# One decoder step on one core: the first tile's experts chosen in three parts, and two of its query products ahead of the other tile's layer norm

## The chip, the cores and the metric

The kernel runs on 1 core of one Trainium2 chip. A core has five engines with instruction streams of their own: TensorE (PE; PEld are its weight loads), VectorE (DVE), ScalarE (ACT), GpSimd (POOL) and SyncE (SP). They meet only at semaphores, and each runs its own list strictly in order. The metric is the device time of one execution in microseconds (us), as the median of several runs.

## The reference

Input are 512 tokens of a prompt and 8 sequences of 8 new tokens, 576 rows of 1024 float32 numbers. One layer is computed: a token mixer (a state-space branch and a sliding-window attention branch, gated and added), then a layer norm, then PEER, a layer with 16,384 experts, then a second layer norm. What matters here is the end of the mixer and PEER:

```
x1 = layer_norm(ALPHA * x + merged @ w_out)
q  = x1 @ peer_wq                      # 8 heads, two halves of 64 each
s1, s2 = q_half1 . k1, q_half2 . k2    # 128 scores each, per token and head
v1, i1 = top_k(s1, 16);  v2, i2 = top_k(s2, 16)
sc, sel = top_k(v1[:, None] + v2[None, :], 16)     # of the 256 pairs
idx, gate = i1 * 128 + i2 at sel, softmax(sc)      # 16 experts per head
h   = peer_u[idx] . x1                 # 8 * 16 = 128 rows of 1024 per token
out = sum(gelu(h) * gate * peer_v[idx])
x2 = layer_norm(ALPHA * x1 + out)
```

So each token fetches 128 rows of `peer_u` and 128 rows of `peer_v`, each of 4 KB.

## The kernel before, in words

**Tiles.** Tile 0 holds the 64 new tokens, tiles 1 to 4 hold 128 prompt tokens each. Tiles 1 and 0 form group 0, whose mixer runs first; tiles 2, 3, 4 form group 1, whose mixer runs while the experts of tiles 1 and 0 are worked on. PEER takes the tiles in the order 1, 0, 2, 3, 4.

**Slots.** A slot is one expert per token. Per slot GpSimd issues one indirect DMA for 128 rows of `peer_u` (`u_row`, L500) and one for `peer_v` (`v_row`, L507), 0.5 MB each, the latter four slots later. Tile 0 is folded onto 128 partitions and has 64 slots, the others have 128: 576 slots in all. VectorE makes the dot product of a u row (L1221), ScalarE the GELU for four slots together (L1471) and a diagonal matrix per slot (L1465), and TensorE adds diagonal times v row into banks 6 and 7 (`weigh`, L795). For a share of the slots VectorE adds the v row itself (L1208, L1211). Four slots make one item `("peer", t, c)`. A u row's place is free again after its dot product, and for the first 72 slots there are 6 places for u rows and 9 for v rows.

**Choosing.** `("sc", t, i)` are the score products of four heads on TensorE (L778), `("top", t, h)` the search for the 16 best pairs of one head on VectorE (L1121 to L1153), and `("choose", t, part)` turns four heads' results into expert numbers and gates on VectorE (L1161 to L1180), with one exponential on ScalarE. `choose` raises the semaphore `idx_s`; GpSimd waits for it before slot 0 and before slot 64 of a tile.

**Order.** `schedule()` writes one list of items, and every engine takes its own work from it in that order (TensorE and part of ScalarE take `peer` items later, behind the items that follow them: `mixer_first`). So the list fixes, on each in-order engine, what stands behind what. Before the first expert it reads: the output product of both tiles (`wo`, L747; on VectorE L1094 and the layer norm, L1078 to L1085), the transposes of the normed tiles (`xt`, L757), four query products for both tiles together (`wq`, L766, 192 columns; ScalarE copies each out, L1271), the scores of the first four heads, the other four query products, four searches, the scores of the second half, and `choose` for 64 slots. After that the list interleaves peer items with group 1: its three query-key-value products (`qkv`, L639 and, on VectorE, L979 to L990), transposes (`turn`, L647), attention scores and their softmax (`s`, L696 and L1042), probabilities times values (`pv`, L713 and L1051), gates, merge, output product and queries.

**Weights.** SyncE loads 104 pieces of 0.5 MB in order of use into a ring of 8 places (L426); a piece waits until the piece that is 8 before it has been used for the last time.

## Time and profile before

| | us |
|---|---|
| median of 3 runs | 2177.97 |
| lowest and highest of them | 2165.36, 2591.91 |
| the profiled execution | 2157.18 |
| span of its instructions | 2155.4 |

| engine | busy us | share of the span |
|---|---|---|
| PE | 1581.4 | 73% |
| DVE | 1370.7 | 64% |
| POOL | 1343.8 | 62% |
| ACT | 387.1 | 18% |

The 16 DMA engines moved 675.05 MB, 609.25 of them in GpSimd's queue (the expert rows and a few small transfers). To read it: the shares are means over stages that differ. Until 347 us no expert row is fetched; from then to the end the expert rows are. The page's line of DMA shares in 40 slices (of 53.9 us each) reads 5234346967999987999899999999989999999997.

### The profile page before, as it was taken

How to read it: one execution, taken by the hardware profiler on the slowest of the kernel's cores; microseconds unless marked ns; L12 is line 12 of the kernel's file. 1: busy time of each engine (PE TensorE's matmuls, PEld its weight loads, DVE VectorE, ACT ScalarE, POOL GpSimd, SP SyncE). 2: the span in 40 equal slices, each digit the busy share in tenths (PEclk: the TensorE clock that was granted, in tenths of full speed). 3: DMA queues.
4: the chain of work that ended last, by engine and by line, in shares of the span. 5: the costliest groups of instructions: out<-in, count | busy, mean ns of one | idle time of the engine just before them, and what ended most of it. 6: DMA issues, size and time to landing. Idle time of an engine off the chain costs nothing.

```text
span 2155.4 us, 16267 instructions
## 1 busy us (share of the span) xinstructions
PE 1581.4 (73%) x4705; PEld 797.3 (37%) x4705; DVE 1370.7 (64%) x3118; ACT 387.1 (18%) x905; POOL 1343.8 (62%) x1370
## 2 busy tenths in 40 slices
PE   6979986776987786876677675766675767776766
PEld 4667853444544332421232232322232322222222
DVE  7551237978989689858775666654476656444444
ACT  0222211223323122001111111111011121111111
POOL 0064004646667665777677777777777777667774
PEclk9979998878998898898889797989887889999998
DMA  5234346967999987999899999999989999999997
GB/s 213 90 78 119 124 141 219 347 216 267 356 367 379 373 310 272 400 351 370 292 371 373 356 371 358 364 383 367 391 328 357 358 356 389 367 362 373 380 369 269
DMA packets 186552, 675.05 MB, mean 313 GB/s; under 512 B 20960, under 2 KB 23440, under 8 KB 186048
## 3 DMA queue, kind: packets, MB, share of 16 engines
q0 software_dynamic: 167056, 609.25, 75.9%
q1 hardware_dynamic: 17632, 59.51, 7.7%
q10 hardware_dynamic: 1776, 5.24, 0.6%
q8 instruction: 39, 0.64, 0.1%
q14 instruction: 49, 0.40, 0.1%
HBM read 669.71 MB, written 3.69 MB: 312 GB/s over the span
## 4 chain that ended last, share of the span: by engine, by line
PE 29%; POOL 20%; issue 18%; DVE 15%; DMA 13%; another core or an unknown queue 2%; ACT 2%; ACTq 0%; SPq 0%; POOLq 0%; DVEq 0%
PE bank L795 15%; POOL region L507 7%; POOL region L500 6%; DMA region<-in_pv,region 6%; PE bank L726 4%; POOL wring L500 4%; DVE region L1221 2%; DMA discretisation<-in_pv,region 2%; DVE region L1211 2%; DMA wring<-in_pv,region 1%; DMA wring<-in_pu,region 1%; PE bank L547 1%; DMA region<-in_pu,region 1%; PE bank L747 1%
## 5 line engine op out<-in xcount | busy, mean ns | idle before, releaser
L795 PE MATMUL bank<-region,small 128*128 128x512 f32 (+1 forms) x1296 | 653.4, 650 | 281.3 <-ACT small L1465 123.0
L500 POOL DMA_INDIRECT region<-in_pu,region x348 | 390.6, 1122 | 292.2 <-DVE region L1221 103.4
L1221 DVE CUSTOM_DVE_ANT_0 region<-region 128x1024 f32<-128x1024 f32 x348 | 424.3, 1227 | 224.8 <-DMA region<-in_pu,region 199.3
L507 POOL DMA_INDIRECT region<-in_pv,region x392 | 442.5, 1129 | 163.3 <-issue 114.0
L795 PEld LDWEIGHTS bank<-region,small 128*128 128x128 f32 (+1 forms) x1296 | 248.8, 202 | 667.0 <-issue 546.0
L1221 DVE CUSTOM_DVE_ANT_0 wring<-wring,region 128x1024 f32<-128x1024 f32 x228 | 276.9, 1226 | 216.0 <-DMA wring<-in_pu,region 186.5
L500 POOL DMA_INDIRECT wring<-in_pu,region x228 | 238.4, 1046 | 69.5 <-issue 69.2
L1465 ACT ACTIVATE small<-small,region 128x128 f32<-128x128 f32 (+1 forms) x480 | 157.2, 387 | 667.5 <-DVE region L1195 241.3
L795 PE MATMUL bank<-discretisation,small 128*128 128x512 f32 (+1 forms) x196 | 117.9, 733 | 124.1 <-issue 65.4
L795 PE MATMUL bank<-wring,small 128*128 128x512 f32 x256 | 119.1, 599 | 22.7 <-DMA wring<-in_pv,region 15.4
L726 PE MATMUL bank<-xT,wring 128*128 128x192 f32 (+1 forms) x512 | 130.7, 417 | 0.0
L1471 ACT ACTIVATE region<-region 128x4 f32<-128x4 f32 x144 | 29.4, 204 | 519.2 <-issue 253.3
L726 PEld LDWEIGHTS bank<-xT,wring 128*128 128x128 f32 x512 | 94.2, 198 | 39.1 <-issue 7.3
L795 PEld LDWEIGHTS bank<-discretisation,small 128*128 128x128 f32 (+1 forms) x196 | 38.8, 213 | 188.5 <-issue 126.8
L1211 DVE SCALAR_TENSOR_TENSOR region<-region 128x1024 f32<-128x1024 f32 x66 | 84.9, 1287 | 18.4 <-issue 17.1
L795 PE MATMUL bank<-small 128*128 128x512 f32 (+1 forms) x172 | 87.6, 634 | 11.4 <-DMA small<-in_pv,region 7.2
L507 POOL DMA_INDIRECT small<-in_pv,region x60 | 68.8, 1146 | 26.1 <-issue 18.8
L507 POOL DMA_INDIRECT wring<-in_pv,region x64 | 69.9, 1093 | 19.5 <-issue 17.1
L507 POOL DMA_INDIRECT discretisation<-in_pv,region x60 | 65.3, 1089 | 25.0 <-issue 14.6
L795 PEld LDWEIGHTS bank<-wring,small 128*128 128x128 f32 x256 | 46.7, 190 | 91.7 <-issue 90.5
L747 PE MATMUL bank<-wring,region 128*128 128x512 f32 (+1 forms) x160 | 72.4, 612 | 9.3 <-DVE region L1069 9.3
L766 PE MATMUL bank<-xT,wring 128*128 128x192 f32 (+1 forms) x256 | 69.7, 433 | 1.4 <-ACT xT L1271 1.4
(244 smaller groups left out, 1709.8 us busy)
## 6 DMA issues: line engine op xcount, KB each, us to landing
wring<-in_w SPq DMA_DIRECT2D x104, 512.0 KB
region<-in_pv,region POOLq DMA_INDIRECT x392
region<-in_pu,region POOLq DMA_INDIRECT x348
wring<-in_pu,region POOLq DMA_INDIRECT x228
out_y<-region ACTq DMA_DIRECT2D x4, 512.0 KB
small<-in_small ACTq DMA_DIRECT2D x1, 1669.0 KB, 14.2
xT<-in_xT SPq DMA_DIRECT2D x1, 1536.0 KB, 20.0
region<-in_x SPq DMA_DIRECT2D x3, 512.0 KB, 16.7
```

The lines of the kernel that those rows point to most:

```text
L500: pool.indirect_dma_start(ring_u[u_at.place[q]], None, io["pu"], bass.IndirectOffsetOnAxis(ind[:, k:k + 1], 0)).then_inc(g_u[u_at.place[q] ...
L507: pool.indirect_dma_start(ring_v[v_at.place[q]], None, io["pv"], bass.IndirectOffsetOnAxis(ind[:, k:k + 1], 0)).then_inc(g_v[v_at.place[q] ...
L547: last = mm(b[:, 0:cn], w[:, k, :], xT[:, k, c0:c0 + cn], start=k == 0, stop=k == KT - 1)
L726: last = mm(b[:, 0:cn], w[:, k0 + k, :], src[:, k, s0:s0 + cn], start=k == 0, stop=k == kn - 1)
L747: last = mm(b[0:tn, :], mTg[g][:, k, rel(t):rel(t) + tn], w[:, 512 * hf:512 * hf + 512], start=k == 0, stop=k == KT - 1)
L766: last = mm(b[:, 0:cn], w[:, k, :], xT[:, k, c0:c0 + cn], start=k == 0, stop=k == KT - 1)
L795: last = mm(bank[6 + hf][0:tn, :], diag[:, d % DIAGS, 0:tn], ring_v[v_at.place[q]][:, 512 * hf:512 * hf + 512], start=k == 0, stop=t not i ...
L1211: V.scalar_tensor_tensor(out=acc, in0=ring_v[v_at.place[q]], scalar=aact[:, n % 2, k:k + 1], in1=acc, op0=ALU.mult, op1=ALU.add).then_inc( ...
L1221: V.tensor_tensor_reduce(out=ring_u[u_at.place[q]], in0=ring_u[u_at.place[q]], in1=x1[t], scale=1.0, scalar=0.0, op0=ALU.mult, op1=ALU.add ...
L1465: S.activation(diag[:, d % DIAGS, 0:tn], eye, ACT.Copy, scale=aact[:, n % 2, k:k + 1]).then_inc(diag_s, 1)
L1471: S.activation(hact[:, n % 2, k], hdot[:, n % 2, k], ACT.Gelu).then_inc(act_s, 1)
```

## The change

The first tile (tile 1) chooses its experts in three parts, of heads 0 and 1, 2 and 3, and 4 to 7, in place of two of four heads. The query products of heads 0 and 1 are made in two pieces: `wqf` for the 128 columns of tile 1, right after its transposes, and `wql` for the 64 columns of tile 0, after its own. The item `wo` is cut into one per half and an item `ln`; tile 0's second output half, its layer norm, transposes and all further query products now stand behind the first `choose` in the list. The weights of the first two query heads get two places of their own (in the region that later holds v rows), and the ring of 8 carries the rest. GpSimd waits before slots 0, 32 and 64 of tile 1. Searches 2 to 7 and two `choose` items of tile 1 now stand between its peer items.

```diff
+CHOICES = {1: [(0, 2), (2, 4), (4, 8)]}
+AHEAD = 2
+AHEAD_PLACES = 7
...
-    s += [("wo", 1), ("wo", 0), ("xt", 1), ("xt", 0)] + [("wq", 0, h) for h in range(4)] + [("sc", 1, 0)]
-    s += [("wq", 0, h) for h in range(4, 8)]
-    s += [("top", 1, h) for h in range(4)] + [("sc", 1, 1), ("choose", 1, 0)]
-
-    first = [[("top", 1, h)] for h in range(4, 8)] + [[("choose", 1, 1)]]
+    s += [("wo", 1, 0), ("wo", 1, 1), ("ln", 1), ("wo", 0, 0), ("xt", 1)] + [("wqf", h) for h in range(AHEAD)] + [("sc", 1, 0), ("wo", 0, 1)]
+    s += [("top", 1, 0), ("top", 1, 1), ("choose", 1, 0), ("ln", 0), ("xt", 0)] + [("wql", h) for h in range(AHEAD)]
+    s += [("wq", 0, 2), ("wq", 0, 3), ("sc", 1, 1)] + [("wq", 0, h) for h in range(4, 8)]
+
+    first = [[("top", 1, 2)], [("top", 1, 3), ("sc", 1, 2)], [("choose", 1, 1)]] + [[("top", 1, h)] for h in range(4, 8)] + [[("choose", 1, 2)]]
...
-                if i >= PIECES:
-                    sp.wait_ge(filled, plan.filled[plan.last_use[pieces[i - PIECES]]])
+                if before_in_slot[p]:
+                    sp.wait_ge(filled, plan.filled[plan.last_use[before_in_slot[p]]])
+                elif p in ahead:
+                    wait_item(sp, ("ht",))
...
-                    if k == 0:
-
-                        pool.wait_ge(idx_s, 2 * n + (2 if t == 0 else 1))
-                    if k == 64:
-                        pool.wait_ge(idx_s, 2 * n + 2)
+                    if t == 0 and k == 0:
+
+                        pool.wait_ge(idx_s, chosen(0, 1))
+                    for p, (h0, h1) in enumerate(choices(t)):
+                        if t and k == TOPK * h0:
+                            pool.wait_ge(idx_s, chosen(t, p))
...
                     if v_at.before[q] is not None:
                         wait_v_used(pool, v_at.before[q])
+                    elif v_at.place[q] in range(AHEAD_PLACES, AHEAD_PLACES + AHEAD):
+                        pool.wait_ge(filled, plan.filled[("wql", AHEAD - 1)])
...
+            def do_wqf(h):
+
+                after(("xt", 1, 1))
+                b = enter(("wqf", h))
+                w = arrived(0, "wq", h).rearrange("p (k n) -> p k n", k=8)
+                for k in range(KT):
+                    last = mm(b[:, 0:128], w[:, k, :], xT[:, k, 64:192], start=k == 0, stop=k == KT - 1)
+                last.then_inc(filled, 1)
...
-            def do_wo(t):
-                tn = TILES[t][1]
-                dve.wait_ge(x2_in if t > 1 else x_in, 16 * len(GROUPS[group(t)]))
-                dve.wait_ge(ln_in, 16)
...
+            def do_wo(t, hf):
+                if hf == 0:
+                    dve.wait_ge(x2_in if t > 1 else x_in, 16 * len(GROUPS[group(t)]))
+                    wo_half(t, 0)
+
+            def do_ln(t):
+                wo_half(t, 1)
+                dve.wait_ge(ln_in, 16)
+                tn = TILES[t][1]
                 layer_norm(x1[t][0:tn, :], x1[t][0:tn, :], tn, ln1).then_inc(x1_s, 1)
...
-                heads, half = slice(4 * part, 4 * part + 4), slice(64 * part, 64 * part + 64)
+                h0, h1 = choices(t)[part]
+                nh, nk, heads, half = h1 - h0, TOPK * (h1 - h0), slice(h0, h1), slice(TOPK * h0, TOPK * h1)
...
-                    step(V.tensor_tensor(eq[0:tn], posf[0:tn, side, half].unsqueeze(2).broadcast_to([tn, 64, TOPK]),
-                                         s("iota")[0:tn].unsqueeze(1).broadcast_to([tn, 64, TOPK]), ALU.is_equal))
+                    step(V.tensor_tensor(same, posf[0:tn, side, half].unsqueeze(2).broadcast_to([tn, nk, TOPK]),
+                                         s("iota")[0:tn].unsqueeze(1).broadcast_to([tn, nk, TOPK]), ALU.is_equal))
...
+            def do_wqf(h):
+                b = full(("wqf", h))
+                drain(("wqf", h), copy(q2T(1, h), b[:, 0:128]))
```

What the list does to the engines' orders is shown at two places. The first is TensorE, from the output products to the end of the qkv products. Before (L747 `wo`, L757 `xt`, L766 `wq`, L778 `sc`, L639 `qkv`, L795 `weigh`):

```order
L747 MATMUL bank<-wring,region 128x512 x16
L747 MATMUL bank<-wring,region 64x512 x16
L757 MATMUL bank<-small,region 128x128 x8
L757 MATMUL bank<-small,region 128x64 x8
L766 MATMUL bank<-xT,wring 128x192 x32
L778 MATMUL bank<-small,region 128x128 x8
L766 MATMUL bank<-xT,wring 128x192 x32
L778 MATMUL bank<-small,region 128x128 x8
L639 MATMUL bank<-wring,xT 128x512 x8
L639 MATMUL bank<-wring,xT 128x256 x8
L795 MATMUL bank<-region,small 128x512 x8
L639 MATMUL bank<-wring,xT 128x512 x8
```

Changed (L783 `wo`, L793 `xt`, L811 `wqf`, L820 `wql`, L802 `wq`, L833 `sc`, L676 `qkv`, L850 `weigh`):

```order
L783 MATMUL bank<-wring,region 64x512 x8
L793 MATMUL bank<-small,region 128x128 x8
L811 MATMUL bank<-xT,region 128x128 x16
L833 MATMUL bank<-small,region 128x128 x4
L783 MATMUL bank<-wring,region 64x512 x8
L793 MATMUL bank<-small,region 128x64 x8
L820 MATMUL bank<-xT,region 128x64 x16
L802 MATMUL bank<-xT,wring 128x192 x16
L833 MATMUL bank<-small,region 128x128 x4
L802 MATMUL bank<-xT,wring 128x192 x32
L676 MATMUL bank<-wring,xT 128x512 x8
L676 MATMUL bank<-wring,xT 128x256 x8
```

Two heads' queries and four score products come ahead; the transposes of tile 0, and with them all other query products and the three `qkv`, come behind the layer norm that VectorE makes after its first `choose`. Between the first and the second `qkv` there now stand 8 score products (`("sc", 1, 2)`), which wait until VectorE has read the two banks in its fourth search.

The second place is ScalarE, around the first GELU of the experts. Before (L1410 the square root of a layer norm, L1271 copies, L1435 the exponential of `choose`, L1471 the GELU):

```order
L1271 ACTIVATE hgT<-bank 128x64
L1271 ACTIVATE region<-bank 128x128
L1435 ACT_TABLE_LOAD
L1435 ACTIVATE region<-region 128x64
L1471 ACT_TABLE_LOAD
L1471 ACTIVATE region<-region 128x4
```

Changed (L1475 the square root, L1336 copies, L1509 the exponential, L1545 the GELU; eight more rows of copies are left out):

```order
L1509 ACT_TABLE_LOAD
L1509 ACTIVATE region<-region 128x32
L1475 ACT_TABLE_LOAD
L1475 ACTIVATE stat<-stat 64x1
L1336 ACTIVATE xT<-bank 128x4x64 x2
L1336 ACTIVATE hgT<-bank 128x64 x3
...
L1336 ACTIVATE hgT<-bank 128x64
L1336 ACTIVATE region<-bank 128x128
L1545 ACT_TABLE_LOAD
L1545 ACTIVATE region<-region 128x4
```

The exponential of the first `choose` now stands ahead of the copies of tile 0 and of the later queries, and the first GELU behind all of them.

## Rows read from the trace of the kernel before

**Rows 1.** Windows: busy us of PE, PEld, DVE, ACT, POOL, clock, DMA share, GB/s.

```profile
347.00:539.00 192.00, 135.34 (x419) 79.79 (x418) 150.94 (x323) 45.80 (x89) 116.38 (x101) 0.80 0.79 287
539.00:755.00 216.00, 176.14 (x497) 95.69 (x495) 189.03 (x404) 58.19 (x82) 142.83 (x124) 0.91 0.98 369
1037.00:2155.00 1118.00, 771.58 (x1615) 308.18 (x1613) 643.46 (x1484) 167.42 (x505) 830.05 (x765) 0.88 0.96 362
```

**Rows 2.** Timeline, GpSimd: start us, us, instruction, [idle before <- what ended it].

```profile
347.47 1.04 POOL L500 DMA_INDIRECT region<-in_pu,region  x1 [81.55 <-DVE region L1180]
```

**Rows 3.** Timeline, VectorE, from the first layer norm to the first dot product.

```profile
278.99 0.69 DVE L1094 SCALAR_TENSOR_TENSOR region<-region,bank 128x512 f32<-128x512 f32 x1 [5.57 <-PE bank L747]
...
285.47 1.22 DVE L1085 TENSOR_TENSOR region<-region 128x1024 f32<-128x1024 f32 x1
...
316.94 0.50 DVE L1121 MAX8 region<-bank 128x8 f32<-128x128 f32 x2 [17.78 <-PE bank L778]
...
336.72 0.23 DVE L1161 TENSOR_TENSOR region<-region 128x64 f32<-128x64 f32 x1
...
337.83 1.23 DVE L1168 TENSOR_TENSOR region<-region,small 128x1024 f32<-128x1024 f32 x1
...
351.89 1.23 DVE L1221 CUSTOM_DVE_ANT_0 region<-region 128x1024 f32<-128x1024 f32 x1 [5.33 <-DMA region<-in_pu,region]
```

**Rows 4.** Timeline, TensorE, from the output products to the first qkv.

```profile
264.87 27.88 PE L747 MATMUL bank<-wring,region 128*128 128x512 f32 x64 [0.91 <-DVE region L1069]
292.68 1.10 PE L757 MATMUL bank<-small,region 128*128 128x128 f32 x8
299.22 1.11 PE L757 MATMUL bank<-small,region 64*128 64x64 f32 x8 [5.44 <-DVE region L1085]
300.86 13.49 PE L766 MATMUL bank<-xT,wring 128*128 128x192 f32 x64 [0.53 <-ACT xT L1271]
315.12 1.68 PE L778 MATMUL bank<-small,region 64*128 64x128 f32 x16 [0.77 <-ACT region L1271]
316.73 10.67 PE L766 MATMUL bank<-xT,wring 128*128 128x192 f32 x64
...
336.20 12.84 PE L639 MATMUL bank<-wring,xT 128*128 128x512 f32 x32
```

**Rows 5.** Windows, TensorE alone, the start of the query products: busy, granted clock, DMA.

```profile
301.00:308.00 7.00, 7.00 (x26) 0.60 0.66 235
```

**Rows 6.** Timeline, ScalarE: the first square root's table, and the first GELU.

```profile
281.64 1.28 ACT L1410 ACT_TABLE_LOAD   x1 [19.74 <-DVE stat L1080]
...
358.74 0.20 ACT L1471 ACTIVATE region<-region 128x4 f32<-128x4 f32 x1 [18.87 <-DVE region L1221]
```

**Rows 7.** Timeline, TensorE: the second qkv, four slots weighed, first scores, 16 small products.

```profile
369.76 10.48 PE L639 MATMUL bank<-wring,xT 128*128 128x512 f32 x32
...
397.08 7.03 PE L795 MATMUL bank<-region,small 128*128 128x512 f32 x16
...
410.24 3.78 PE L696 MATMUL bank<-region 64*128 64x256 f32 x8 [1.36 <-ACT region L1271]
...
498.86 1.93 PE L713 MATMUL bank<-region 128*64 128x128 f32 x16 [2.64 <-ACT region L1271]
```

**Rows 8.** Timeline, VectorE: dots after the first and third qkv, the third's addition, first attention scores.

```profile
379.63 1.23 DVE L1221 CUSTOM_DVE_ANT_0 region<-region 128x1024 f32<-128x1024 f32 x1 [0.46 <-issue]
...
402.33 0.69 DVE L979 TENSOR_TENSOR region<-bank,small 128x512 f32<-128x512 f32 x1
...
405.19 1.22 DVE L1221 CUSTOM_DVE_ANT_0 region<-region 128x1024 f32<-128x1024 f32 x1
...
416.58 1.42 DVE L1042 SCALAR_TENSOR_TENSOR region<-bank,small 128x512 f32<-128x512 f32 x2
```

**Rows 9.** Waits of VectorE, 431 to 539 us: total us, times, longest.

```profile
DVE region L1051 <- PE bank L713: 3.9, 3, 1.3
DVE region L1042 <- PE bank L696: 3.4, 5, 1.4
```

More of the change, by code:

```diff
@@ L55, in n_slots, with choices, part_of, chosen @@
     return 64 if t == 0 else 128
+def choices(t):
+    return CHOICES.get(t, [(0, 4), (4, 8)])
+def part_of(t, h):
+    return next(p for p, (h0, h1) in enumerate(choices(t)) if h0 <= h < h1)
+def chosen(t, p):
+    return sum(len(choices(o)) for o in ORDER[:ORDER.index(t)]) + p + 1
 def schedule():
@@ L161, in item_jobs @@
     if k == "wo":
-        return [(("wo", a[0], hf), "D", [(a[0] > 1, "wo", i) for i in range(8)]) for hf in range(2)]
+        return [(("wo", *a), "D", [(a[0] > 1, "wo", i) for i in range(8)])]
     if k == "xt":
@@ L215, in hybrid_step @@
     pieces = plan.pieces
-    piece_no = {p: i for i, p in enumerate(pieces)}
+    slot_of, nth_of, before_in_slot, holds = {}, {}, {}, {}
+    ahead = [(0, "wq", h) for h in range(AHEAD)]
+    for i, p in enumerate(pieces):
+        slot = PIECES + ahead.index(p) if p in ahead else (i - sum(q in ahead for q in pieces[:i])) % PIECES
+        slot_of[p], before_in_slot[p] = slot, holds.get(slot)
+        nth_of[p] = nth_of[holds[slot]] + 1 if slot in holds else 1
+        holds[slot] = p
     ctx = ExitStack()
@@ L776, in do_sc @@
                     b = enter(("sc", t, side, i))
-                    for h in range(4):
-                        last = mm(b[0:tn, 128 * h:128 * h + 128], q2T(t, 4 * i + h)[rows], k12[rows, 4 * i + h, :],
+                    for h in range(h0, h1):
+                        last = mm(b[0:tn, 128 * (h - h0):128 * (h - h0) + 128], q2T(t, h)[rows], k12[rows, h, :],
                                   start=True, stop=True)
@@ L1487, in _ @@
                     "turn": do_turn, "ss": do_ss, "pvs": do_pvs, "s": do_s, "pv": do_pv, "gates": do_gates, "merge": do_merge,
-                    "wo": do_wo, "xt": do_xt, "wq": do_wq, "choose": do_choose, "fold": do_fold, "before": do_before, "peer": do_peer, "last": do_last,
+                    "ln": do_ln, "xt": do_xt, "wq": do_wq, "wqf": do_wqf, "wql": do_wql, "choose": do_choose, "fold": do_fold, "before": do_before, "peer": do_peer, "last": do_last,
                     "final": do_final}
```

109 lines of the change are left out of this document (65 added, 44 removed).

## The prediction

> **What bounds the kernel now.** I read first the windows of all engines by stage, to see where a delay or a lead is kept. From 1037 us to the end the DMA engines are 96% busy at 362 GB/s, and from 539 to 755 us 98% at 369 GB/s [rows 1]: there the expert rows are the bound, and the reader sees that no engine is nearly as busy in the long last stage. From 347 to 539 us the DMA share is only 0.79, while VectorE is busy 150.9 of 192 us: here GpSimd issues as fast as VectorE frees the six places of u rows, and VectorE frees them only at the points of its list where dots stand. So the kernel has three pieces in series: a prelude without expert rows to 347 us, a stretch paced by VectorE's list to about 539 us, and a long one paced by transfers. The order and number of dots, and the places, are the same in both kernels from 539 us on, so whatever lead VectorE's list has there is a lead at the end. The question is what is left of it at 539 us.
>
> Then the timelines of the prelude. The first expert row is issued at 347.47 us, when `choose` is done [rows 2]. Ahead of it stand, one behind the other, the output products of both tiles (27.88 us), two layer norms, transposes, four query heads in 13.49 us, scores, four searches from 316.94 to 336.72 us (4.95 us each) and `choose` [rows 3, 4].
>
> **The prelude, step by step.** Tile 1's layer norm ends at 285.47 + 1.22 = 286.7 us in both kernels: the output half before it arrives when it did [rows 3]. TensorE, busy with the third half until 264.87 + 3 x 6.97 = 285.8 us, can then transpose [rows 4]. Transposes and copies took 300.86 - 299.22 = 1.64 us for tile 0; I take 2.2 us for the double width, and reach 288.9 us. The two ahead heads are 32 matmul records with 128 columns. No row has just that; the nearest is 16 in 1.93 us [rows 7], so 3.9 us; the other end is double, 7.7 us, if the clock has fallen. I take 3.9, since TensorE has paused only some 1 and 1 us. Copy and half of the score product's 1.68 us add 1.2: searches begin at 294.0 us instead of 316.94. Two searches, 9.9 us. From the start of `choose` to the first row 10.75 us passed (336.72 to 347.47); six of its operations have 1024 elements, at 1.23 us, and now 512, for which the nearest row has 0.69 us: 10.75 - 6 x 0.54 = 7.5 us [rows 2, 3]. First expert row: 294.0 + 9.9 + 7.5 = **311.5 us, 36.0 us earlier**.
>
> Then VectorE finishes tile 0: half an output addition, 0.69 us, and a layer norm that takes what tile 1's took, 286.69 - 279.68 = 7.0 us, so from 310.6 to 318.3 us [rows 3]. That hides the flight of the first rows, which took 4.4 us. First dot at 318.3 instead of 351.89, 33.6 us earlier.
>
> **What is put behind it.** Tile 0's layer norm ended at 299.2 us before, since its transposes start at 299.22 [rows 4], and ends at 318.3 now, 19.1 us later. All of this hangs on it, on TensorE, in order: transposes and copies 1.6 us; 32 records with 64 columns, at 1.11 us for 8, 4.4 us; six heads at 10.67 / 4 = 2.67 us, 16.0; scores 0.84 + 0.77 of waiting, 1.6 us; and a start at the low clock, for which I take what the first four heads lost to the last four, 13.49 - 10.67 = 2.8 us [rows 4]. That ends at 344.7 us. The granted clock was 0.60 in the first 7 us after the 5.4 us pause, so between the two levels of 1.2 and 2.4 GHz [rows 5]; the new pause, from 301 to 318 us, is longer. *The Trainium skill, "TensorE: Matmul & The Clock Gate", Part 1, speaks against the change here: an array left idle falls to 1.2 GHz and has to earn 2.4 back. The trace agrees, with its 0.60. Without that rule the sum would be 2.8 us lower.*
>
> The first `qkv` takes 10.48 us at speed [rows 7] and ends at 355.2 us; before, 336.20 + 12.84 = 349.0 [rows 4]. So TensorE delivers it **6 us later than before**, while VectorE could want it 30 us earlier.
>
> ScalarE has a new wait, too. Its first GELU stood free before, and idled 18.87 us for VectorE [rows 6]. Now it stands behind the copies of all queries in ScalarE's list. So it runs at 344.7 + 0.6 + a table load of 1.28 = 346.6 us, and VectorE, which multiplies that GELU with the gates after its fifth dot, stops from about 325 to 347 us. Queued behind it: three dots, a search, the first rotary; and on GpSimd the u rows beyond the eleventh. This costs nothing of its own as long as TensorE's `qkv` ends at 355.2 us: 347 + 3.6 + 4.95 = 355.5. If that cover went, it would be the bound for 20 us.
>
> *The Trainium skill, "ScalarE: Activation LUTs", section "What ACT_TABLE_LOAD costs", counts some 2.66 us for a switch of table with its drain. The layer norm I copied from holds one such load, and its row has 1.28 us [rows 6]. By the page the layer norm of tile 0 would be 1.4 us longer, and the sum too; I take the row.*
>
> **From there to 539 us.** Addition and rotary are 405.19 - 402.33 = 2.9 us, of which 2.2 behind the last product [rows 8]. First rotary done at 358.0 us (21 us ahead of the 379.63 of before). Four dots, about 5 us: 363.2. Now the new 8 score products of the third part wait until the fourth search has read the banks, 1.5 us into it, 364.7 us (TensorE has weighed by 362.2 and idles), 1.7 us, then the second `qkv`: 376.9. Three slots weighed, 5.3 us; third `qkv` to 392.7; rotary done at 394.9 instead of 405.19: **10.3 us ahead**. VectorE itself would have come to it at 379.1 + 5 + 6.6 = 390.7, so TensorE bounds. Four slots weighed, 7.0, to 399.7 us; transposes and first scores followed 414.0 - 404.1 = 9.9 us behind that, the first half of them some 2 earlier [rows 7]: attention starts at about 408.7 us, **7.9 us ahead** of 416.58 [rows 8].
>
> In the attention steps VectorE's list now holds more than before. In place of `choose` for 64 slots (9.85 us) the first step has a search (4.95): 4.9 gained, of which 2 are lost to a wait for probabilities times values. Two more searches, 9.9, which cover waits for TensorE; those were 7.3 us in all [rows 9], and I let 5.5 be covered. Then `choose` for 64 slots, 9.85. Sum: 7.9 + 4.9 - 2.0 - 9.9 + 5.5 - 9.85 = -3.5 us. The lead is used up, and VectorE comes to 539 us **some 3.5 us later than before**.
>
> Costed at nothing: the loads of the two ahead heads (issued right behind the output pieces that TensorE reads from 265 us on, used at 289), the extra exponential and table loads between peer items (ScalarE is busy 46 of 192 us [rows 1]), GpSimd's wait for `wql` before its eighth v row (it is over at 324 us, and that row is GpSimd's 19th from 311.5 us on, at over 1 us each [rows 2]).
>
> **Sum.** 2157.18 + 3.5 = 2160.7 us against the profiled execution. The median of the three runs is 2177.97, 20.8 us above it; against that it is 2181.5. I cannot tell which of the two a new median resembles, and predict the middle, **2170 us**.
>
> **Rivals.**
> *The lead survives (0.21).* If TensorE does not hold VectorE up, the lead is 33.6 less the moved work (two searches 9.9, the small `choose` 6.6) plus 5.5 of covered waits: 22.6 us, 2135 against the profile, 2145 against the middle. For it: VectorE was the busiest engine until 539. Against it: the transposes of tile 0 are 19 us later, and everything on TensorE hangs on them. All 36 us (2121) would need the moved work hidden as well: 0.03.
>
> *TensorE's chain is longer, and the kernel slower (0.21).* Each restart after a wait runs at the low clock: 2.4 us (12.84 against 10.48) at the second and third `qkv`, 3.8 for the ahead heads, and the searches cover none of the 5.5: 14.1 + 3.5 = 17.6 us, 2175, or 2185 against the middle. It decides from the point where the fourth search starts after TensorE has weighed its first slots, at 362 us; my numbers have it 1 us beyond.
>
> *The ahead heads do not come ahead (0.05).* If their weights, which SyncE issues behind the eight output pieces, landed only at 297 us, all later points shift by 8 us: 2169, or 2179.
>
> The forecast itself, within 8 us of its sum, has 0.50. The range takes the surviving lead against the profile at its low end and the longer chain against the median, 2174.8 + 20.8, at its upper: **2136 to 2198 us**. A change of less than 2%, 43 us, is not told from none here. The first row comes only 36 us earlier, so faster by over 2% needs luck in the runs: 0.04; slower by over 2% as well: 0.04; within: 0.92.
>
> **What would show it.** First expert row near 311 us, first dot near 318. The gate product of VectorE waiting about 20 us for ScalarE's first GELU, and GpSimd idle meanwhile. The first `qkv` starting near 345 us, after 336 before. First attention scores near 409 us, and tile 0's first search near 543 us, 539.59 before. I am wrong if that last point comes before 530 us, or if the DMA share after it falls below what it was.

## The result, and the profile after

Over 20 runs of each kernel the changed kernel takes 2170.43 us in the median (2160.78 to 2195.61), the kernel before 2165.86 (2145.23 to 2591.91). The ratio is 1.0048, 95% interval [1.0025, 1.0071]: within 2%, and still a real loss, of 5 to 15 us. It leaves out, here and below, slow executions, over 1.5% above the fastest of their kernel (2591.91 us is one); the means of the others are 2172.3 and 2162.2 us, 10.0 us apart, where the medians of all 20 are only 4.6 us apart. A repeat in ten runs gave 1.0035 [1.0005, 1.0065], 7.6 us. The profiled execution took 2164.40 us (span 2162.6); before it was 2157.18 (2155.4).

The windows of the changed kernel, to hold against [rows 1] (busy us of PE, PEld, DVE, ACT and POOL, then clock, DMA share, GB/s):

```profile
347.00:539.00 192.00, 144.48 (x434) 84.03 (x433) 158.64 (x377) 49.85 (x93) 94.59 (x81) 0.80 0.67 235
539.00:755.00 216.00, 175.66 (x511) 97.29 (x510) 185.92 (x401) 56.95 (x82) 147.24 (x123) 0.90 0.97 368
1037.00:2155.00 1118.00, 774.90 (x1620) 308.25 (x1620) 637.96 (x1478) 168.57 (x508) 822.47 (x768) 0.88 0.96 362
```

From 539 us on the stages look as they did. Between 347 and 539 us VectorE has 8 us more to do, and the DMA share falls from 0.79 to 0.67: GpSimd issues fewer rows there (81 against 101), since the others went ahead.

GpSimd's first row and VectorE's prelude (start us, us, [idle before <- what ended it]), to hold against [rows 2, 3]:

```profile
306.84 1.03 POOL L536 DMA_INDIRECT region<-in_pu,region  x1 [46.80 <-DVE region L1146]
```
```profile
279.60 1.22 DVE L1140 TENSOR_TENSOR region<-region 128x1024 f32<-128x1024 f32 x1
...
289.66 0.49 DVE L1184 MAX8 region<-bank 128x8 f32<-128x128 f32 x2 [8.13 <-PE bank L833]
...
299.55 0.19 DVE L1225 TENSOR_TENSOR region<-region 128x32 f32<-128x32 f32 x1
...
308.77 0.15 DVE L1137 RECIPROCAL stat<-stat 64x1 f32<-64x1 f32 x1 [0.27 <-ACT stat L1475]
...
312.31 1.22 DVE L1286 CUSTOM_DVE_ANT_0 region<-region 128x1024 f32<-128x1024 f32 x1
```

Tile 1's norm ends at 280.82 us here and at 286.69 before. That is no effect of the change: over all profiled executions it ends between 280.8 and 286.7, and in two kernels that differ from the one before only behind this point (less and delay, below) it ends at 280.90 and 285.10. So every point below is counted **from the end of tile 1's layer norm**. First row at 26.0 us (60.8 before), first dot at 31.5 (65.2).

TensorE, to hold against [rows 4, 7]:

```profile
282.85 5.47 PE L811 MATMUL bank<-xT,region 128*128 128x128 f32 x32 [0.88 <-ACT xT L1336]
...
312.33 1.11 PE L793 MATMUL bank<-small,region 64*128 64x64 f32 x8 [15.81 <-DVE region L1140]
313.98 7.09 PE L820 MATMUL bank<-xT,region 128*128 128x64 f32 x32 [0.53 <-ACT xT L1336]
320.86 7.14 PE L802 MATMUL bank<-xT,wring 128*128 128x192 f32 x32
332.48 1.23 PE L833 MATMUL bank<-small,region 64*128 64x128 f32 x8 [4.47 <-issue]
333.63 12.80 PE L802 MATMUL bank<-xT,wring 128*128 128x192 f32 x64
346.27 10.48 PE L676 MATMUL bank<-wring,xT 128*128 128x512 f32 x32
...
366.66 1.68 PE L833 MATMUL bank<-small,region 64*128 64x128 f32 x16 [3.04 <-DVE region L1190]
```

and VectorE behind it, to hold against [rows 8]:

```profile
348.61 0.16 DVE L1260 TENSOR_TENSOR region<-region 128x4 f32<-128x4 f32 x1 [28.94 <-ACT region L1545]
...
377.20 0.69 DVE L1034 TENSOR_TENSOR region<-bank,small 128x512 f32<-128x512 f32 x1 [7.07 <-PE bank L676]
...
409.11 1.42 DVE L1097 SCALAR_TENSOR_TENSOR region<-bank,small 128x512 f32<-128x512 f32 x2
...
543.52 0.49 DVE L1184 MAX8 region<-bank 64x8 f32<-64x128 f32 x2 [1.78 <-PE bank L833]
```

VectorE starts its dots 34 us earlier and then stands still for 28.9 us behind a GELU, which stands behind all query copies. Attention starts at 128.3 us (129.9 before): a lead of 34 us has become 1.6. Tile 0's first search starts at 262.7 us (252.9 before), 9.8 us late, about as much as the loss in time.

Where the last part comes from is seen in two windows, from the first attention scores to tile 0's first search, before (the first row) and after:

```profile
416.60:539.60 123.00, 83.82 (x279) 52.42 (x278) 98.04 (x154) 36.66 (x64) 65.65 (x56) 0.77 0.70 246
```
```profile
409.00:543.50 134.50, 91.49 (x280) 56.38 (x279) 112.19 (x229) 36.66 (x64) 65.08 (x56) 0.71 0.65 227
```

VectorE has 14.2 us more work in it (112.19 against 98.04), and idles 22.3 us in place of 25.0: the stretch is 11.5 us longer. For the change to gain anything, attention would have to start more than 11 us earlier than before.

### The profile page after: what moved, and what is told of

The parts are those of the page before. It is cut to its first block, busy times and chain, and to the rows that moved or that the text cites. A ratio compares the mean times of both kernels' runs of the same rounds, so it can differ in the third digit from the quotient of the medians.

```text
span 2162.6 us, 16365 instructions
## 1 busy us (share of the span) xinstructions
PE 1583.5 (73%) x4737; PEld 800.5 (37%) x4737; DVE 1371.1 (63%) x3134; ACT 390.8 (18%) x909; POOL 1338.1 (62%) x1370
## 4 chain that ended last, share of the span: by engine, by line
PE 31%; POOL 24%; issue 17%; DVE 14%; DMA 11%; ACT 2%; another core or an unknown queue 2%; ACTq 0%; SPq 0%; DVEq 0%; POOLq 0%
PE bank L850 16%; POOL region L545 8%; POOL region L536 7%; DMA region<-in_pv,region 6%; POOL wring L536 5%; PE bank L763 4%; PE bank L676 2%; DVE region L1286 2%; PE bank L802 1%; POOL wring L545 1%; PE bank L584 1%; POOL small L545 1%; DMA region<-in_pu,region 1%; DMA wring<-in_pv,region 1%
## 5 line engine op out<-in xcount | busy, mean ns | idle before, releaser
L850 PE MATMUL bank<-region,small 128*128 128x512 f32 (+1 forms) x1296 | 655.4, 653 | 321.6 <-issue 189.0
L536 POOL DMA_INDIRECT region<-in_pu,region x348 | 384.3, 1104 | 281.6 <-DVE region L1286 125.1
L850 PEld LDWEIGHTS bank<-region,small 128*128 128x128 f32 (+1 forms) x1296 | 251.4, 202 | 707.7 <-issue 598.9
L850 PE MATMUL bank<-discretisation,small 128*128 128x512 f32 (+1 forms) x196 | 112.4, 701 | 95.2 <-issue 59.7
L850 PE MATMUL bank<-wring,small 128*128 128x512 f32 x256 | 120.0, 601 | 18.6 <-DMA wring<-in_pv,region 13.7
L763 PE MATMUL bank<-xT,wring 128*128 128x192 f32 (+1 forms) x512 | 130.9, 417 | 0.0
L1545 ACT ACTIVATE region<-region 128x4 f32<-128x4 f32 x144 | 29.4, 204 | 498.2 <-DVE region L1286 273.8
L850 PE MATMUL bank<-small 128*128 128x512 f32 (+1 forms) x172 | 89.4, 644 | 9.6 <-DMA small<-in_pv,region 6.9
L850 PEld LDWEIGHTS bank<-discretisation,small 128*128 128x128 f32 (+1 forms) x196 | 37.7, 207 | 157.4 <-issue 119.5
L1276 DVE SCALAR_TENSOR_TENSOR region<-region 128x1024 f32<-128x1024 f32 x66 | 84.9, 1286 | 14.2 <-issue 13.0
L545 POOL DMA_INDIRECT wring<-in_pv,region x64 | 75.5, 1179 | 28.2 <-issue 17.7
L783 PE MATMUL bank<-wring,region 128*128 128x512 f32 (+1 forms) x160 | 72.9, 615 | 9.1 <-DVE region L1124 9.1
L850 PEld LDWEIGHTS bank<-wring,small 128*128 128x128 f32 x256 | 46.2, 189 | 89.6 <-issue 88.0
L763 PE MATMUL bank<-hgT,wring 128*128 128x192 f32 (+1 forms) x256 | 67.6, 420 | 2.7 <-issue 2.7
## 6 DMA issues: line engine op xcount, KB each, us to landing
small<-in_small ACTq DMA_DIRECT2D x1, 1669.0 KB, 14.2
```

The costliest lines, as they stand in the source:

```text
L536: pool.indirect_dma_start(ring_u[u_at.place[q]], None, io["pu"], bass.IndirectOffsetOnAxis(ind[:, k:k + 1], 0)).then_inc(g_u[u_at.place[q] ...
L545: pool.indirect_dma_start(ring_v[v_at.place[q]], None, io["pv"], bass.IndirectOffsetOnAxis(ind[:, k:k + 1], 0)).then_inc(g_v[v_at.place[q] ...
L763: last = mm(b[:, 0:cn], w[:, k0 + k, :], src[:, k, s0:s0 + cn], start=k == 0, stop=k == kn - 1)
L783: last = mm(b[0:tn, :], mTg[g][:, k, rel(t):rel(t) + tn], w[:, 512 * hf:512 * hf + 512], start=k == 0, stop=k == KT - 1)
L850: last = mm(bank[6 + hf][0:tn, :], diag[:, d % DIAGS, 0:tn], ring_v[v_at.place[q]][:, 512 * hf:512 * hf + 512], start=k == 0, stop=t not i ...
L1276: V.scalar_tensor_tensor(out=acc, in0=ring_v[v_at.place[q]], scalar=aact[:, n % 2, k:k + 1], in1=acc, op0=ALU.mult, op1=ALU.add).then_inc( ...
```

## The experiments

Points in us from the end of tile 1's norm, read from each kernel's timeline; ratios to the kernel before on the same chip. Chips differ: the kernel before has its median at 2162 to 2166 us on some and at 2089 to 2090 on others, so only points and ratios are compared. The points and the span are those of the one profiled execution. What lies behind tile 0's search takes 1616 to 1628 us in the executions with a span near 2160, and 1535 to 1558 us in those near 2090, whatever the order: these differences are larger than the effects looked for, so the time is read from the ratios. (after: the changed kernel.)

| run | first row | tile 0 normed | first qkv | attention | tile 0's search | span | ratio, 95% |
|---|---|---|---|---|---|---|---|
| before | 60.8 | 12.5 | 49.5 | 129.9 | 252.9 | 2155.4 | 1 |
| before_again | 60.8 | 12.5 | 49.5 | 129.0 | 252.7 | 2090.1 | one execution |
| after | 26.0 | 31.5 | 65.4 | 128.3 | 262.7 | 2162.6 | 1.0048 [1.0025, 1.0071] |
| after_again | 24.4 | 29.8 | 58.3 | 122.3 | 254.0 | 2093.1 | one execution |
| after_more | 24.4 | 29.8 | 65.3 | 129.2 | 260.9 | 2160.7 | 1.0035 [1.0005, 1.0065] |
| hold | 24.4 | 29.8 | 58.3 | 129.4 | 262.6 | 2164.7 | 1.0088 [1.0059, 1.0117] |
| fill | 26.0 | 31.5 | 58.7 | 121.5 | 255.9 | 2094.5 | 1.0026 [0.9989, 1.0064] |
| gelu | 24.4 | 29.8 | 56.7 | 118.6 | 252.9 | 2093.2 | 1.0025 [0.9992, 1.0058] |
| ln0 | 30.8 | 23.5 | 61.0 | 125.4 | 259.4 | 2164.7 | 1.0001 [0.9966, 1.0037] |
| sclate | 26.0 | 31.5 | 65.8 | 123.8 | 255.9 | 2165.1 | 1.0017 [0.9985, 1.0048] |
| both | 26.0 | 31.5 | 65.7 | 123.7 | 256.8 | 2155.8 | 1.0010 [0.9975, 1.0044] |
| three | 45.5 | 12.5 | 41.6 | 128.6 | 262.6 | 2161.3 | 1.0004 [0.9967, 1.0041] |
| three_more | 45.7 | 12.5 | 41.8 | 125.8 | 259.7 | 2084.4 | 1.0032 [0.9993, 1.0071] |
| three_sclate | 45.6 | 12.5 | 41.6 | 118.1 | 252.4 | 2151.2 | 0.9987 [0.9958, 1.0016] |
| best | 41.3 | 12.5 | 55.7 | 116.4 | 249.2 | 2162.3 | 0.9973 [0.9945, 1.0001] |
| best_more | 41.3 | 12.5 | 55.4 | 116.3 | 249.2 | 2080.9 | 0.9993 [0.9958, 1.0027] |
| delay | 60.8 | 12.5 | 49.5 | 126.7 | 266.6 | 2086.4 | 1.0070 [1.0037, 1.0102] |
| less | 60.4 | 12.5 | 49.1 | 129.8 | 255.2 | 2079.8 | 0.9995 [0.9954, 1.0035] |

### Is a loss at tile 0's search a loss at the end?

**delay**, in the kernel before:

```diff
-                for side in range(2):
+                for side in (0, 1) * (1 + (2 if (t, part) == (1, 1) else 0)):
```

> The kernel before with the passes over pairs of positions in tile 1's second choice done three times in place of once (results the same): twice 7.55 us more on VectorE inside the attention stretch, nothing else. Theory 1 (VectorE's arrival at tile 0's first search sets the end one for one): the stretch from tile 1's norm to it grows from 252.8 to 266 to 268 us, time +13 to +15 us, ratio 1.006 to 1.007. Rival (the experts' part behind it takes the loss back, since it runs by its own transfers and clock): stretch as long, ratio within 1.002.

The search came 13.9 us later than in before_again (266.6 against 252.7), the time grew by 0.70%, 14.6 us with an interval of 8 to 21. The rival (the rest takes it back) is out: the step on which the whole sum rests, a loss there is a loss at the end, holds as far as this interval tells. The one profiled execution does not show it by itself: its span, 2086.4, is below the 2090.1 of before_again.

**three_more** (the three parts alone, repeated) asked the same of an order that had not fitted: three had a search as late as the changed kernel's, 262.6, yet 1.0004.

> The three parts alone once more, unedited. Its stretch was 262.6 us, 9.8 longer than before's, yet its time 1.0004 [0.9967, 1.0041]. Theory 1: the first run sat at the low end of its own uncertainty; now 1.002 to 1.005, stretch 260 to 263. Rival (with rows of the first part still at 45 us after the norm the rest is shorter, so the stretch doesn't decide): again within 1.001.

Now 1.0032 at 259.7 us. Its interval still reaches 1, and the two of three overlap; a search 7 to 10 us late is worth 0.3 to 0.5% here too, as far as these runs can tell. The points do not give the whole time, though: hold (below) has its search 9.9 us late and loses 13 to 25 us.

### Is VectorE's work ahead of attention worth anything?

**less**, in the kernel before; heads 4 to 6 of tile 1 are not searched:

```diff
             def do_top(t, h):
+                if (t, h) in ((1, 4), (1, 5), (1, 6)):
+                    step(V.tensor_copy(i16[0:128, :, h], i16[0:128, :, 3]))
+                    step(V.tensor_copy(top[0:128, h], top[0:128, 3]))
+                    step(V.tensor_copy(pos[0:128, h], pos[0:128, 3]))
+                    return
                 top_keys(t, h)
```

> The kernel before without the searches of heads 4, 5 and 6 of tile 1: head 3's results are copied in their place, so this part of the computation is left out. Three searches of 4.9 us less and nine small copies of some 0.15 us more, -13 us of VectorE's work, two of the three ahead of attention's first scores. Theory 1: part of it turns into waits for TensorE (the keys' and values' products, 2 to 5 us), stretch 241 to 245 us in place of 252.8, time -8 to -12 us, ratio 0.994 to 0.996. Rival (a lead at tile 0's first search is not a lead at the end): stretch as short, ratio 0.998 to 1.001.

Both theories missed: the search did not come earlier at all (255.2), and the time is 0.9995 [0.9954, 1.0035], where 13.4 us less would be 0.9936. All three searches stand ahead of attention, not two. VectorE's waits from 340 to 410 us, before_again and then less (total, times, longest):

```profile
DVE region L1221 <- DMA region<-in_pu,region: 13.3, 6, 5.7
```
```profile
DVE region L1226 <- DMA region<-in_pu,region: 23.6, 13, 5.5
DVE region L981 <- PE bank L639: 2.8, 1, 2.8
```

VectorE works 13.4 us less in those 70 (busy 40.27 against 53.66) and waits 10.3 + 2.8 us more. **Before attention the kernel before waits for rows and for the qkv products; searches there cost nothing.** In the attention steps work costs its length: in delay 15.1 us of it cost 13.9. The change moved three searches from the one place to the other, 14.8 us, and these are about the 14.2 us of more work above.

### The stall on TensorE

**after_again and before_again** repeated both kernels on a faster chip.

> The changed kernel, unchanged, a second profile. The same interval was 543.52 - 280.82 = 262.7 us. If the stretch of 4.5 us in which TensorE stood idle between the fourth query head and the scores (328.0 to 332.5 us) belongs to the kernel, it comes again and the interval is 262 to 263; if it was chance of one execution, the interval is about 259.

> The kernel before, unchanged, a second profile. I measure from the end of tile 1's layer norm to tile 0's first search: 539.59 - 286.69 = 252.9 us in the first profile. Both theories expect 251 to 255 us again, and the end of that layer norm itself anywhere between 280 and 288 us, since the two profiles so far differ by 5.9 us there with the same instructions ahead of it.

There the fourth query head is followed by the scores after 0.73 us in place of 4.47, and the last four heads take 10.67 in place of 12.80. The search came at 254.0 us, earlier than either expectation: without the stall the change loses only 1.3 us there. How much of the time it loses on such a chip was not measured. **after_more** asked when it happens.

> The changed kernel once more, unedited, beside the three that follow, for the size of its loss on one chip and for TensorE's stall. Two of its profiled executions differ: in the first TensorE stood 4.5 us between its fourth query head and the scores, ran the last four heads in 12.8 us, and attention began 128.3 us after the end of tile 1's layer norm; in the second there was no such stall, 10.7 us and 122.3 us. The stall was in three of three profiles of programs with span near 2163 us (the changed kernel, the scores moved, tile 0's norm first) and in none of three with span near 2093. Theory 1 (it belongs to the slower chips, whose expert rows fill the DMA queues while TensorE's instructions are still to be fetched): with a span near 2160 the stall of 4 to 5 us returns and the stretch from the norm to tile 0's first search is 260 to 263 us; with a span near 2093 it is absent and the stretch is 254 us. Theory 2 (it comes and goes by execution): either span can show either. In both, time over the kernel before: 1.001 to 1.005.

With a span of 2160.7 the stall is back (4.96 us, heads in 13.16 us, first qkv at 65.3), as theory 1 expected for such a span. It stood in the profiles of after, sclate, both and after_more, in ln0 as several short stops, and in none of after_again, fill and gelu: five of five near 2160, none of three near 2093. **hold** keeps most early rows back:

```diff
+HOLD = 5
...
+                    if q == HOLD:
+                        pool.wait_ge(filled, plan.filled[("wq", 0, 7)])
```

> GpSimd holds its rows from the sixth place on until TensorE has finished the last query head; the first five u rows and one v row go at once, as before. Theory 1 (early expert rows fill the DMA queues and hold up what TensorE needs, instructions or data): no stall of 4 us behind the fourth head even on a slower chip, first key and value product 58 us after tile 1's norm and not 65, attention at 122, tile 0's first search at 254 to 256. The clock low at the first 64-column heads stays, since the pause is the same. Theory 2 (the stall has another cause): on a chip on which the changed kernel beside this one shows it, it stands here as well, 4 to 5 us. Time against the kernel before: theory 1 1.000 to 1.003; theory 2 1.002 to 1.006.

TensorE in hold (same chip as after_more):

```profile
321.43 8.01 PE L805 MATMUL bank<-xT,wring 128*128 128x192 f32 x32
330.17 0.72 PE L836 MATMUL bank<-small,region 64*128 64x128 f32 x8 [0.73 <-ACT region L1339]
330.82 10.67 PE L805 MATMUL bank<-xT,wring 128*128 128x192 f32 x64
341.33 10.48 PE L679 MATMUL bank<-wring,xT 128*128 128x512 f32 x32
```

and in after_more:

```profile
328.71 0.65 PE L802 MATMUL bank<-xT,wring 128*128 128x192 f32 x3 [1.24 <-issue]
334.31 1.23 PE L833 MATMUL bank<-small,region 64*128 64x128 f32 x8 [4.96 <-ACT region L1336]
335.48 13.16 PE L802 MATMUL bank<-xT,wring 128*128 128x192 f32 x64
```

Without the rows the stall is gone and the first qkv is 7 us earlier, at a DMA share of 0.31 in place of 1.03 (321 to 333 us): the early expert rows, or GpSimd's issuing of them, which this edit holds back as well, cause it. The lead was lost again, since VectorE then waited 7.1 us for the rows held, and TensorE 10.5 us for VectorE's fourth search; so the guess at attention (122) missed. So did both guesses at the time: 1.0088, 19 us, is twice what the search's 9.9 us explain, and the other half is open. What exactly the rows hold up is open, too: in the stalled kernel (here after) ScalarE also waited for something that the profile cannot name and calls `remote`:

```profile
331.84 0.22 ACT L1336 ACTIVATE hgT<-bank 128x64 f32<-128x64 f32 x1 [5.81 <-remote]
```

Stops of that name are not new with the change. Waits for `remote` stand in all ten profiles with a span between 2151 and 2165 us, of whatever order, and in none of the eight between 2080 and 2095. The earliest of each comes when expert rows are already on the way. In the kernel before VectorE has 16 of them, 37.9 us in all, the first from 1185 us on in the middle of a search (the first line below), and ScalarE 27. In three_sclate (below) VectorE meets them in its fourth search (the second line):

```profile
1187.35 0.09 DVE L1149 MATCH_VALUE_LOAD region<-region 128x8 f32 x1 [2.29 <-remote]
```
```profile
370.18 0.09 DVE L1212 MATCH_VALUE_LOAD region<-region 128x8 f32 x1 [1.67 <-remote]
```

So the stall looks like one of these stops, which by bad luck of the place hits the chain that everything waits for. That it is the same thing was not shown.

### The low clock: fill

```diff
+FILL = 17
...
+                if t == 0:
+                    after(("wqf", AHEAD - 1))
+                    for i in range(FILL):
+                        mm(bank[6][:, :], ident, xT[:, 0, 64:576], start=True, stop=True)
```

> The changed kernel, with 17 extra products (512 columns, into a bank nobody reads) on TensorE in the gap before tile 0's transposes. Theory 1, the chain on TensorE behind tile 0's layer norm bounds, and restarts at the low clock: the two wql heads take 4 us instead of 7.1, the six others 16 instead of 19.9, the first qkv starts 6 to 7 us earlier, and the interval to tile 0's first search shrinks by 5 to 7 us, the time as much. Theory 2, VectorE's own work is the bound: the first qkv starts earlier but the interval stays within 1.5 us.

Windows of fill, the filling products, then tile 0's two heads, then the next two:

```profile
296.00:311.00 15.00, 15.00 (x36) 6.38 (x34) 13.89 (x40) 3.00 (x4) 3.28 (x4) 1.00 0.91 323
314.00:320.50 6.50, 6.50 (x32) 6.50 (x32) 4.56 (x8) 0.25 (x2) 5.28 (x5) 0.50 0.95 357
320.50:329.00 8.50, 7.77 (x40) 7.38 (x40) 0.00 (x0) 1.20 (x5) 6.37 (x8) 0.78 0.97 362
```

TensorE was busy at 1.00 until 1 us ahead of the transposes, and these still ran at 1.00. Yet it got 0.50, the 1.2 GHz level, for the 64-column heads: 0.66 in their first 1.4 us, 0.50 in the rest. They took 6.74 us in place of 7.09, not 4. So the long pause is not what makes them slow; the clock fell while they ran, behind two pauses of 1.0 and 0.6 us. Which of the two, the short pauses or the narrow products, took it down is open. The prediction leaned on the Trainium skill, "TensorE: Matmul & The Clock Gate", Part 1, for the pause; here filling it bought 0.4 us at these heads and 1.2 us in the whole chain up to the first qkv (27.3 us in place of 28.5 in after_again), not 6 to 7. With so little gained, this run does not decide between its two theories.

### The waits one at a time: gelu, ln0, sclate

**gelu** puts the last four heads, and so their copies, behind the first search among the peer items:

```diff
-... ("sc", 1, 1)] + [("wq", 0, h) for h in range(4, 8)]
+... ("sc", 1, 1)]
-    first = [[("top", 1, 2)], ...
+    first = [[("top", 1, 2)] + [("wq", 0, h) for h in range(4, 8)], ...
```

> The changed kernel with the last four query heads put behind the second peer item in the list, so that ScalarE's first GELU no longer stands behind their copies. VectorE's stop of 28.9 us at its first gate product shrinks to 12 to 16 us. Theory 1, TensorE's chain bounds: the first qkv ends at the same time, and interval and time stay within 1.5 us. Theory 2, the stop for the GELU is what costs: the interval shrinks by 6 us or more, and the kernel is as fast as before the change.

VectorE's wait for the GELU fell from 23.2 us (after_again) to 9.6, further than expected. Its waits for the first halves of the qkv products rose from 8.2 us, at the second one, to 15.5: 8.5 at the first and 7.1 at the second. Attention came 3.7 us earlier and the search 1.1. The GELU wait was hidden, all but 1 to 4 us of it.

**ln0** puts tile 0's norm and transposes ahead of the first `choose`:

```diff
-... ("choose", 1, 0), ("ln", 0), ("xt", 0)] + ...
+... ("ln", 0), ("xt", 0), ("choose", 1, 0)] + ...
```

> The changed kernel with tile 0's layer norm and transposes put ahead of the first choose in the list (behind the two searches). All points counted from the end of tile 1's layer norm. Theory 1, TensorE's chain bounds: tile 0's layer norm ends at 24 us instead of 30 to 31.5, the first qkv starts at 51 to 58 instead of 58 to 65, the first expert row comes at 31 instead of 24 to 26, and tile 0's first search comes 4 to 6 us earlier than in the changed kernel, at 249 to 257. Theory 2, the first expert row sets the pace: everything, the last point too, is 6 us later, 260 to 268.

First row 5 to 6 us later, tile 0's norm 6.3 to 8.0 us earlier, and with it the first qkv 4.3 and the search 1.5 to 3.3 us earlier than in after_more and after: rows are not what is waited for, tile 0's norm is. Its ratio is lower than its search says (259.4), by no more than its interval.

**sclate** puts the third part's scores behind the second qkv:

```diff
-    first = [[("top", 1, 2)], [("top", 1, 3), ("sc", 1, 2)], [("choose", 1, 1)]] + ...
+    first = [[("top", 1, 2)], [("top", 1, 3)], [("sc", 1, 2), ("choose", 1, 1)]] + ...
```

> The changed kernel with the score products of the third part put behind the second group-1 qkv, so that TensorE no longer waits for the fourth search in front of it. Theory 1: TensorE's wait of 3.0 us and 1.7 us of products leave the place ahead of that qkv, first attention scores come 2 to 4 us earlier and so does tile 0's first search (250 to 259 us after tile 1's layer norm). Theory 2, VectorE's own work is the bound: within 1 us of the changed kernel.

TensorE's 3.04 us wait for VectorE's search is gone, attention 4.5 us and the search 6.8 us earlier than in after: theory 1, and somewhat more than it asked for.

### The parts alone and together: three, three_sclate, both, best

**three** keeps the three parts and puts no head ahead (the lines that these replace are left out):

```diff
+AHEAD = 0
...
+    s += [("wo", 1, 0), ("wo", 1, 1), ("ln", 1), ("wo", 0, 0), ("wo", 0, 1), ("ln", 0), ("xt", 1), ("xt", 0)]
+    s += [("wq", 0, 0), ("wq", 0, 1), ("sc", 1, 0), ("wq", 0, 2), ("wq", 0, 3)]
+    s += [("top", 1, 0), ("top", 1, 1), ("sc", 1, 1)] + [("wq", 0, h) for h in range(4, 8)] + [("choose", 1, 0)]
```

> The three-part choice alone: tile 0's output half, layer norm and transposes stand where they stood before the change, all query products are made for both tiles, the first choose comes after two heads. Counted from the end of tile 1's layer norm: first expert row at about 41 us (before the change 60.8, changed 24 to 26), first qkv at about 41 to 45 (49.5; 58 to 65). Theory 1: the wait for the fourth search ahead of the second qkv still costs, first attention scores at about 119, and the moved searches take it back: tile 0's first search at 252 to 256, no gain over the 252.8 of before. Theory 2, the start of the expert rows sets the pace: 20 us less than before, some 233.

**three_sclate** is three with sclate's edit.

> The three-part choice alone, and the third part's score products behind the second qkv. Theory 1, VectorE's waits for TensorE are what used up the lead: now the second and third qkv are ready when VectorE comes, first attention scores at about 109 us after tile 1's layer norm (129 before the change), tile 0's first search at 243 to 247, so 6 to 10 us less than before, and the time 5 to 10 us below the kernel before. Theory 2, the lead is used up by VectorE's moved work alone: as three, within 1.5 us.

three has its first qkv 24 us before the changed kernel's, and yet its search as late: VectorE waits 8.5 us for the second qkv, which stands behind the third part's scores. With these moved (three_sclate) attention starts at 118.1 us, 11 us earlier than before the change, and the search at 252.4 is level with before, as the 11.5 us above demand. Both runs missed their expectations: attention and search came some 10 and 7 us or more too late in three, 9 and 5 us or more in three_sclate, and no run shows why.

**both** is the changed kernel with gelu's and sclate's edits.

> The changed kernel with both earlier edits together: the last four query heads behind the first search that stands with attention's side, and the third choice's scores behind the second key and value product. Theory 1 (what counts is when attention starts, against some 11 us more of searches and choices that the stretch to tile 0's first search now holds): the edits gave 3.7 and 4.5 us, so attention starts at 114 to 120 us after the norm, tile 0's first search at 248 to 253, level with or ahead of the kernel before (252.8), time 0.998 to 1.001 of it. Rival (the rest of the execution is longer with these orders, as after the moved scores alone, 1628 us of rest against 1616): the stretch is as short but the time is 1.002 or more.

Two edits did not add (attention at 123.7, as in sclate alone, search at 256.8, both past the expectation): with the stall TensorE's first qkv is at 65.7 whatever ScalarE does. **best** is three_sclate with the last four heads behind the first search among the peer items and `choose` ahead of the second part's scores.

> Three parts of choices with no head ahead of the rest (both transposes, then all heads), the first choice ahead of the second part's scores so that its Exp does not stand behind the query copies, the last four heads behind the first search that stands with attention's side, and the third part's scores behind the second key and value product. Theory 1: the three parts with the moved scores had attention at 118.1 and tile 0's first search at 252.4 us after the norm, 0.9987 of the time; VectorE's waits there for Exp (4.5 us) and for the first rows shrink, so attention at 113 to 118, first search at 247 to 252, time 0.996 to 0.999. Rival (a lead at tile 0's first search is not a lead at the end, since the experts' part runs by its own DMA and clock): first search as early, time 0.999 to 1.002.

> The order with 0.9973 [0.9945, 1.0001] once more, unedited. Theory 1: its stretch of 249.2 us is 3.6 shorter than before's, worth 0.0017: ratio 0.996 to 0.999, stretch 247 to 251. Rival: 0.999 to 1.002, the first ratio having been low by chance.

Attention and search repeat to 0.1 us, 116.4 and 249.2, 3.6 us ahead of before. That is worth 0.17%, which lies in both intervals; neither shows it faster, and the second ratio lies where the rival had it.

## Why the prediction was right, and where it was wrong

**Class and number.** No change of 2%, as forecast, but the direction was wrong. The number on record, 2170 us, lies 8 us below the 2177.97 it stood beside, a small gain; measured is a loss of 5 to 15 us. Two steps made that. The last one took a middle between the profiled 2157 and the three runs' 2178, though the working before it had found 3.5 us of loss against either. That 2170 stands beside a median of 2170.43 is luck: the median of the kernel before fell to 2165.86 with more runs. The other step is the sum itself: 3.5 us, where the ratios say 10.4 and 7.6 and the search of tile 0 came 9.8 and 8.0 us late. (Small slips beside these: the middle is 2171, and by its own terms the range would be 2135 to 2196.)

**The prelude was right.** From the norm's end: first row predicted at 24.8 us, measured 26.0 and 24.4; tile 0 normed and first dot 31.6, measured 31.5 and 29.8. The two ahead heads took 5.47 us in place of 3.9. For the table load of tile 0's norm the prediction had an estimate of 1.4 us more from the Trainium skill, "ScalarE: Activation LUTs", section "What ACT_TABLE_LOAD costs". The load ran ahead of need, VectorE waited 0.27 us for it, and this trace shows no such cost.

**The step that failed: TensorE's chain behind tile 0's norm**, from 318.3 to 344.7 us, 26.4 us in the prediction and 34.0 in the first profile. It has two parts. Without the stall (after_again) the chain is 28.5 us, from 312.6 to 341.1: the 64-column heads took 7.09 us in place of 4.4, the next two 8.01 in place of 5.3, against one allowance of 2.8 for the low clock. The stall and the second run at low clock behind it make the other 5.5. The lines of after_again:

```profile
314.35 7.09 PE L820 MATMUL bank<-xT,region 128*128 128x64 f32 x32 [0.53 <-ACT xT L1336]
321.23 8.01 PE L802 MATMUL bank<-xT,wring 128*128 128x192 f32 x32
```

The prediction priced this chain from a stretch without expert rows in flight, and never asked what they would do to it; the rival of a longer chain named the low clock, not this cause. The trace of the kernel before could have raised the question, with its 16 stops of VectorE under expert rows, though its own later query products, with the DMA share at 0.98 from 880 to 965 us, took 5.4 to 5.7 us each without a stop inside (7.2 the first). The consequence: attention was predicted at 122.0 us from the norm, 7.9 ahead; it is 6.7 ahead without the stall (122.3 against 129.0) and 1.6 or level with it. That 122.3 fits so well is partly luck: the chain was 2.1 us too long there and tile 0's norm 1.8 us early. From the first qkv to attention the working was right, 64.0 us, measured 62.9 and 64.0.

**The attention steps were right in sum.** Predicted 11.35 us longer; 11.5 in the first profile, and 131.7 to 134.4 us against 123.0 and 123.7 in every order with three parts that was profiled. Of the waits for TensorE of 7.3 us [rows 9] 2.3 are left, so 5.0 were covered where 5.5 were forecast:

```profile
DVE region L1106 <- PE bank L750: 1.3, 1, 1.3
DVE region L1097 <- PE bank L733: 1.0, 1, 1.0
```

**Together** the search was predicted at 256.4 us: 254.0 without the stall, 262.7 and 260.9 with it. The stall is the term that was left out; where it is absent, the sum errs by 2.4 us to the other side.

**The GELU wait** was predicted at 20 us and hidden: 28.9 with the stall, 23.2 without, and hidden but for 1 to 4 us. **The surviving lead**, the rival with 0.21, failed where the forecast put it: VectorE could have been early, TensorE was not. **That no engine works off a lead after 539 us** was shown in one direction by delay; for a lead of 3.6 us the runs are too coarse.

## What to carry to other kernels

A lead at the first transfer is worth what is left of it at the point where the pace is next set; walk the list to that point before believing it. Work moved out of a prelude is free where the engine would wait anyway (the searches ahead of attention) and costs its length where it is the pacer (among the attention steps); some 40 us apart in the same list, the price of 13 to 15 us of work went from nothing (less) to 13.9 us (delay). And transfers that start earlier run under work that had the queues to itself: count that work's time again.

## What was not expected of the hardware

- With the DMA engines full of early expert rows (share 0.99 to 1.03 at 321 to 333 us) TensorE stopped for 4.5 to 5.2 us, or several times for less (ln0), in all five executions with a span near 2160 us that had such rows, and in none of three near 2093, where the share was 0.99 to 1.03 as well. Full queues alone are not enough. Waits that the profile calls `remote` divide the eighteen profiles in the same way, ten with and eight without.
- Products with 64 columns, 32 of them, ran at the granted clock of 0.50 behind 15 us at 1.00, with pauses of 1.0 and 0.6 us between.
- The same program differs by 3.5% between chips (2089.06 and 2162.41 us for the kernel before), and by up to 6 us before 287 us from one execution to the next.
